# State-space scan over strides of four steps, with its matrices built in the feed-forward parts, in a three-layer model on one core

## What is computed

```python
lam_bar = exp(lam * delta)                    # 64 groups x 64 complex states, diagonal
b_bar   = ((lam_bar - 1) / lam)[..., None] * b   # 64 states from 16 channels
state_t = lam_bar * state_{t-1} + b_bar @ u_t # 272 steps
y_t     = real(c @ state_t) + d * u_t         # 16 channels from 64 states
g       = gelu(y);  out = g * sigmoid(g @ w_glu + b_glu)
```

## Time and profile before

| | us |
|---|---|
| median of 3 runs (lowest, highest) | 3449.91 (3440.37, 3450.88) |
| the profiled execution's own time | 3458.53 |
| its span | 3456.4 |
| PE busy, PEld busy | 3290.6 (95%), 2918.0 (84%) |
| DVE, ACT, POOL busy | 1871.3 (54%), 1418.2 (41%), 732.3 (21%) |

### The profile page before, as it was taken

How to read it: one execution, slowest core, us unless ns; L and a number is a source line. 1 busy time by engine, 2 the same in 40 slices (tenths; PEclk the granted TensorE clock), 3 DMA queues, 4 the chain that set the end, 5 groups by cost and what they waited for, 6 DMA issues and landing times.

```text
span 3456.4 us, 53985 instructions
## 1 busy us (share of the span) xinstructions
PE 3290.6 (95%) x20542; PEld 2918.0 (84%) x20542; DVE 1871.3 (54%) x2405; ACT 1418.2 (41%) x2093; POOL 732.3 (21%) x754
## 2 busy tenths in 40 slices
PE   6989999999999998999999999977778999999999
PEld 6977898989898996799998989865545898989897
DVE  4535544444445544554444445599956545454444
ACT  4334543334345434443333333544335433333343
POOL 2100030303031100012121213257731030303030
PEclk9987999999999998899999999987768999999999
DMA  5541445554554453255555554522102455455544
GB/s 192 181 184 37 180 185 195 189 191 180 194 195 176 178 191 122 93 188 188 184 188 194 189 188 182 210 87 74 49 25 88 181 193 189 180 192 194 192 176 167
DMA packets 41616, 567.02 MB, mean 164 GB/s; under 512 B 4512, under 2 KB 4640, under 8 KB 7168
## 3 DMA queue, kind: packets, MB, share of 16 engines
q1 hardware_dynamic: 39536, 557.49, 44.0%
q0 software_dynamic: 704, 4.68, 0.4%
q10 hardware_dynamic: 1232, 2.88, 0.2%
HBM read 562.93 MB, written 2.10 MB: 163 GB/s over the span
## 4 chain that ended last, share of the span: by engine, by line
PE 83%; DVE 8%; issue 5%; ACT 2%; POOL 1%; DMA 0%; ACTq 0%; DVEq 0%; POOLq 0%; SPq 0%
PE bank L549 82%; DVE mprod L1585 1%; DVE w_lo L1303 1%; DVE mprod L1591 1%; DVE zr L1598 1%; DVE ph L1569 1%; DVE zi L1599 1%; DVE ph L1564 1%; PE bank L596 1%; DMA raw<-stream 0%; PE bank L734 0%; POOL cssb L1833 0%; DVE nsum L1664 0%; ACT prob L1062 0%; PE bank L862 0%
## 5 line engine op out<-in xcount | busy, mean ns | idle before, releaser
L549 PE MATMUL bank<-xg_hi,w_hi 128*128 128x256 f32 (+1 forms) x4352 | 1232.6, 283 | 8.4 <-DVE w_lo L1303 6.3
L549 PE MATMUL bank<-xg_lo,w_hi 128*128 128x256 f32 (+1 forms) x4352 | 1233.1, 283 | 0.0
L549 PE MATMUL bank<-xg_hi,w_lo 128*128 128x256 f32 (+1 forms) x4352 | 1232.1, 283 | 0.0
L927 ACT ACTIVATE w_hi<-raw 128x1024 fp32r<-128x1024 f32 x552 | 554.1, 1051 | 877.3 <-PE bank L549 877.0
L1297 DVE TENSOR_TENSOR w_lo<-raw,w_hi 128x1024 fp32r<-128x1024 f32 x480 | 572.6, 1235 | 557.4 <-ACT w_hi L938 557.1
L549 PEld LDWEIGHTS bank<-xg_hi,w_hi 128*128 128x128 f32 x4352 | 829.4, 191 | 24.4 <-issue 21.2
L549 PEld LDWEIGHTS bank<-xg_hi,w_lo 128*128 128x128 f32 x4352 | 830.8, 191 | 0.0
L549 PEld LDWEIGHTS bank<-xg_lo,w_hi 128*128 128x128 f32 x4352 | 824.4, 189 | 0.7
L938 ACT ACTIVATE w_hi<-raw 128x1024 fp32r<-128x1024 f32 x480 | 482.5, 1053 | 764.7 <-PE bank L549 764.7
L549 PE MATMUL bank<-w_hi,act_hi 128*128 128x512 f32 x1920 | 749.7, 390 | 14.9 <-DVE act_lo L1677 13.1
L549 PE MATMUL bank<-w_lo,act_hi 128*128 128x512 f32 x1920 | 748.0, 390 | 0.0
(11 more groups left out here) (277 smaller groups left out, 2044.2 us busy)
## 6 DMA issues: line engine op xcount, KB each, us to landing
raw<-stream SPq DMA_DIRECT2D x264, 2048.0 KB, 7.7
x<-xrow ACTq DMA_DIRECT2D x4, 512.0 KB, 13.4
gfb<-gfin POOLq DMA_DIRECT2D x2, 1024.0 KB, 5.5
out<-x SPq DMA_DIRECT2D x4, 512.0 KB, 6.5
cbias_sb<-cbias SPq DMA_DIRECT2D x2, 768.0 KB, 9.6
bm<-bmat POOLq DMA_DIRECT2D x1, 1024.0 KB, 6.7
cm<-cmat POOLq DMA_DIRECT2D x1, 1024.0 KB, 13.4
tab<-tables ACTq DMA_DIRECT2D x1, 768.0 KB, 5.0
```

The costliest lines, as they stand in the source:

```text
L549: return pe.matmul(o, a, b, start=start, stop=stop, skip_group_check=True)
L927: act.activation(hi[j][:, 8 * h:8 * h + 8, :], raw[r][:, 8 * h:8 * h + 8, P * j:P * j + P], ACT.Copy)\
```

## The change

1. **A stride of four steps.** The scan runs over 68 strides, not 272 steps. For each group of 4 pairs (one channel tile i) five things are needed: a drive matrix (4 inputs into the state, 2x4x[128,128]), sine, cosine and decay of 68 angles for the 4 pairs, a matrix of the inputs within the stride (`near`, 4x[128,128]) and a read-out of the state before the stride (`far`, 2x4x[128,128]). d*u goes into `near`.
2. **These tables are built in the FFN parts.** In each of the two first layers, after the mixer, POOL computes powers and constants (`ssm_powers`, 69 steps that each wait for the one before; ACT's exponentials, sine and cosine stand in `widened` of the output projection, and DVE has one reciprocal); then in each FFN part POOL builds the tables of one i (`ssm_build`, 22 such steps): the first before the FFN's hidden tiles, the others after those of the part before. ACT makes sine and cosine ahead of `ups`. Behind `ups` PE does 8 transposes and 8 matmuls, DVE adds d, ACT copies the results out; SP stores 3376 floats a partition (1.7 MB) to DRAM and loads 0.66 MB of inputs for the next. The constants at the start are gone.
3. **The loop of the second block** has 20 slots, one whole projection tile each (8 u, 2 k, 2 v, 8 q). Slot s also holds `drive(s-1)`, `read_out(s-3)` and DVE's and POOL's work on group s-1 (the same operations as for one pair before, on 272 elements, without the angles). `u` goes to DRAM and comes back in the layout of the stride (one store and four loads from ACT's queue, with ACT waiting for the store), and so does y. SP loads each group's tables (0.52, 0.42 and 0.79 MB).
4. **GELU** moves to slots 14 to 17, in 8 operations per step over strided views; the squares of the queries and their sums go into the slots, tile by tile.
5. **Attention part:** the gate's half tiles stand in steps -2 to 5. The norm of the SSM half runs in steps 9 to 17, its sums by PE. The sums for the attention half are made by PE per tile; its root, scaling and parts stand ahead of ACT's and DVE's splits of the output projection, which PE begins with the SSM half.

The diff, cut to its core:

```diff
+STRIDE = 4
+NQ = L2 // STRIDE
+PT = 4
+MT = STRIDE * NQ
@@ sync
+                def store_tables(i):
+                    sp.wait_ge(tabs_out, i + 1)
+                    sp.dma_start(stabs[i][:, 0:TAB_F], tabs[:]).then_inc(tabs_stored, 16)
+                    sp.dma_start(stabs[i][:, TAB_F:TAB_ALL]..., fmat[:, :, :, 1:POWERS, :]...).then_inc(tabs_stored, 16)
...
+            for s in range(1, 10):
+                if s + 1 < T2:
+                    sp.wait_ge(bu_done, s)
+                    load_drive(s + 1)
+                if s % 2 == 1:
+                    chunk((s + 1) // 2 + 2)
+                if 0 <= s - 2 and s + 1 < T2:
+                    sp.wait_ge(state_ready, s - 1)
+                    load_trig(s + 1)
+                if 0 <= s - 3 and s - 1 < T2:
+                    sp.wait_ge(y_done, s - 2)
+                    load_readout(s - 1)
@@ tensor
+            def ssm_tables(i):
+                pe.wait_ge(mats_ready, i + 1)
+                for e in range(2):
+                    for j in range(PT):
+                        pe.transpose(bank[4 + e][:, P * j:P * j + P], gmat[:, e, j, :], ident)
+                for j in range(PT):
+                    for e in range(2):
+                        last = mm(bank[6][:, P * j:P * j + P], sb_re_im[:, e, j, :], fmat[:, e, j, 0:STRIDE, :]..., e == 0, e == 1)
+                last.then_inc(mats_built, 1)
...
                 ups(T0, n)
+                if i0 is not None:
+                    ssm_tables(i0)
                 widened(T0 + T_UP, 0, None, hidden_ready(0))
...
+            def drive(i):
+                pe.wait_ge(u_landed[i % 2], 64 * (i // 2) + 64)
+                pe.wait_ge(drv_landed[i % 2], 16 * (i // 2) + 16)
+                if i >= 2:
+                    pe.wait_ge(bu_out, i - 1)
+                for e in range(2):
+                    for j in range(PT):
+                        last = mm(bank[4 + 2 * (i % 2) + e][:, NQ * j:NQ * j + NQ], drv[i % 2][:, e, j, :], u[:, i, NQ * j:NQ * j + NQ], True, True)
+                last.then_inc(bu_done, 1)
...
+            for s in range(SLOTS):
+                tile(T, s % 2, s % 2, ...)
+                if s == 0:
                     spread(4)
+                if 1 <= s < T2 + 1:
+                    drive(s - 1)
+                if 3 <= s < T2 + 3:
+                    read_out(s - 3)
...
             pe.wait_ge(kn_ready, 2)
-            for s in range(H2 + 3):
+            for s in range(GLU0, H2 + 3):
+                if 0 <= s - GLU0 < 8:
+                    gate_half((s - GLU0) // 2, (s - GLU0) % 2)
@@ scalar
-            act.activation(dl[:], par_at("log_step", 0, PAIRS), ACT.Exp).then_inc(ssm_exp, 1)
-            ...
             split(0, 0, 0, 0)
...
+            def feed(i):
+                act.wait_ge(evac_done, evacuated(T_B2 + i))
+                act.dma_start(urow[i], us[i % 2][:]...).then_inc(us_stored, 16)
+            def feed_back(i):
+                act.wait_ge(us_stored, 16 * i + 16)
+                for r in range(STRIDE):
+                    act.dma_start(u[32 * r:32 * r + 32, i, :]..., turned[r]).then_inc(u_landed[i % 2], 16)
...
+            for s in range(SLOTS):
+                split_after(T_B2 + s)
+                if s < T2:
+                    feed(s)
+                if 4 <= s < T2 + 4:
+                    y_out(s - 4)
+                if s < T2:
+                    feed_back(s)
+                if 4 <= s < T2 + 4:
+                    y_back(s - 4)
@@ vector
+            for s in range(SLOTS):
+                if s < K0:
+                    input_tile(s)
...
+                split_after(T_B2 + s)
+                if s < 2 * NC:
+                    final_normed(s)
+                if 1 <= s < T2 + 1:
+                    products(s - 1)
+                    driving(s - 1)
+                    sums(s - 1)
@@ gpsimd
                 pool.wait_ge(olo_ready, OTHERS * l + OTHERS)
                 pool.wait_ge(onlo_ready, HB * l + HB)
-                pool.tensor_tensor(scratch, eps, eps, ALU.add)
+                ssm_powers(l)
+                ssm_build(FCH * l)
+                for f in range(FCH - 1):
+                    hidden(T0 + T_FFN, l * H_LAYER, f)
+                    ssm_build(FCH * l + f + 1)
+                hidden(T0 + T_FFN, l * H_LAYER, FCH - 1)
+                pool.wait_ge(tabs_stored, 32 * FCH * l + 32 * FCH + 1)
                 pool.dma_start(gfb[:], gfin).then_inc(gfb_landed, 16)
-                ffn(T0 + T_FFN, l * H_LAYER)
```

More of the change, by code:

```diff
@@ L92 @@
 _at = 0
[L93 removed]
+for _n, _w in [("ident", P), ("halves", P), ("cos", S), ("sin", S), ("mask", 384), ("dist", 384), ("steps", 68), ("live", 68),
+               ("eye4", 32)]:
     TABLES[_n] = (_at, _w)
@@ L115, in mixed_tile, with build @@
     return g + 8 if g < 8 else g - 8
-def build(nc, stream, params, tables, tables2, cbias, xrow, gfin, metaT, bmat, cmat, out):
+def build(nc, stream, params, tables, tables2, cbias, xrow, gfin, metaT, smat, out, stabs, urow, yrow):
     at = [(nc.sbuf_base + 63) // 64 * 64]
@@ L178, in build @@
     tab2 = tab[:, a2:a2 + NTAB2]
-    dist2, steps = tab2[:, 0:416], tab2[:, 416:NTAB2]
-    region = [free_at, free_at + 30 * 4 * S]
+    dist2 = tab2[:, 0:416]
+    region = [free_at, free_end]
     sqj = [place(f"sqj{i}", [P, W], where=region) for i in range(2)]
-    xgf = [place(f"xgf{i}", [P, W], where=region) for i in range(2)]
     diag = place("diag", [P, 2, P], where=region)
@@ L622, in widened @@
                         if n is not None and c and t == 0:
+                            if c == 1 and tables is not None:
+                                pe.wait_ge(tabs_out, tables)
                             pe.wait_ge(evac_done, evacuated(Tb + 4 * c - 1))
@@ L1824, in _ @@
             pool.wait_ge(tab_landed, 16)
-            with pool.Fori(0, DEPTH) as l:
+            for l in range(DEPTH):
                 T0 = l * TILES_LAYER
@@ L1997, in small_params @@
     put("ssm2_g", columns(a["ssm_out_g_2"][0]))
-    put("ssm_d", columns(a["ssm_d_2"][0]))
+    put("ssm_d4", np.tile(a["ssm_d_2"][0].reshape(PAIRS, 32).T, (STRIDE, 1)))
     put("b_glu", columns(a["b_glu_2"][0]))
```

979 lines of the change are left out of this document (576 added, 403 removed).

## The result

The changed kernel took 3406.3 us (median of 4 runs, 3396.1 to 3410.2) against 3450.4 us (median of 4, 3440.4 to 3455.9): a ratio of 0.9871, 95% interval [0.9851, 0.9892], 1.3% faster. The forecast was 3326 us (3.6% faster) with a range of 3292 to 3378: the sign was right, the gain a third of the forecast, the time 80 us above it and outside the range. The profiled execution after took 3396.1 us (span 3394.3 us) where my sum stood at 3334.6 us; these 61.5 us are what has to be explained.

What follows compares the result with a forecast made beforehand. It took the kernel as PE-bound with one 250 us DVE-bound SSM stretch. 3458.5 - 148 (stage 412 to 264) - 7.5 (start) + 17.6 (PE tables) + 12 (POOL late) + 2 (sine) = 3334.6, times 0.9975: 3326 us, range 3292 to 3378.

Steps and rivals of the forecast that it cites:

- Slots 0 to 8: Second block's new loop: first slot 6 us, seven more at 10.3, and 2 for the lead-in, 80 us.
- slots 9 to 12: Second block's new loop: four slots with read-outs or k's small matmuls at 7.5 us each, 30 us.
- each waits for the others in order; I take 10.3: Slot time in the new loop: PE, DVE, ACT and u's round trip lie between 8.6 and 9.8 us; 10.3 taken.
- (10.4 + 8.6) / 2: New loop: u there 10.4 us after its tile, PE asking one tile (8.6 us) later, so a slot is 9.5 us.
- I take 0.13: Small 68-column matmuls on PE at 0.13 us each: 8 for the drive 1.0 us, 12 for the read-out 1.6.
- Rival (a): Slots bound by u's transfer, 8 us longer, at half clock: 13 to 16 us a slot, 3345 to 3366 us; chance 0.25.
- Slots 13 to 19: Seven slots with a q tile, 5.5 us plus 0.3 of sums each, 41 us, and 6 us of GELU uncovered.
- attention to the output projection: Second block's attention: gate halves, steps with gate 31 us, ten without gate 52 at lost clock, and the tail: 107 us.
- Start: Kernel start without the constants: ACT's first split at 17 us instead of 25.89, -7.5 us.
- Tables on PE: FFN parts: 16 small matmuls or transposes and a wait on PE, 2.2 us eight times, +17.6 us, uncovered.
- GpSimd late: First table build of each layer delays POOL's first hidden tile for DVE: 6 us, twice, +12 us (0 to 70).
- rival (c): POOL late in the first FFN parts and PE's table work dearer, each stop 5 us more: 3400 to 3440 us; chance 0.08.

Runs made afterwards that it cites:

- e10: e4 with u collected a slot later, its dependent work another slot later, weights asked for before tables, GELU one slot later, PE's FFN loop written out: 3352.4 us, ratio 0.9702.
- e4: e3 with the drive, products, read-out and copy of y one slot later, so u has a whole slot for its trip: 3360.3 us.
- e1: Changed kernel with both turns of u and y through DRAM left out, so the output differs: 3389.9 us.
- e3: Changed kernel with ACT copying y of slot s-4 before it splits the next weight tile, arithmetic kept: 3374.6 us.
- e12: e10 with spare matmuls in attention steps 13 to 17, PE's FFN loop kept as a loop and sixteen 16-column matmuls ahead of it: 3365.2 us, ratio 0.9742.
- e6: e4 with ACT waiting for no store of its own slot, and PE's FFN loop over the second and third part written out: 3373.7 us.
- e8: e4 with ACT waiting for no store of its own slot, and one transpose replacing PE's table-building work in the FFNs, output wrong: 3344.7 us.
- e9: e4 with ACT waiting for no store of its own slot, and table loads cut to 16 KB once buffers are filled, output differs: 3355.1 us.

## Why the prediction was wrong

**Slots 0 to 8: 92.8 us, forecast 80; slots 9 to 12: 62 us, forecast 30.** (Slots 0 to 8 end here at the k tile of 2342.5.) This is the step that failed, 45 of the 66 us by which the stage was longer (329.7 us by the forecast's own marks, against 264). What failed was "each waits for the others in order; I take 10.3": I set the sums of four engines beside each other and added a little, without walking through ACT's order. There the read-out's bank hangs on a copy behind a split that waits for PE's tile. And I priced a gap at its own length; it costs its length and then several us at half clock. Nor is "(10.4 + 8.6) / 2" a sum: PE asks for u one tile later in every slot, so a round trip of 10.4 gives 10.4 a slot.

PE's own work was mis-sized too, and that the whole 110 lies near e10's 107.1 without waits is luck. "I take 0.13" for a small float32 matmul: each of them makes two entries of 0.11 us in the trace at full clock, so the twenty cost 4.4 us and not 2.6, and a full slot costs PE 10.5 us and not 8.6 (e4, the row at 2287.60, PE busy 10.50 at clock 1.00). Slots 9 to 12, forecast at 7.5 each, took 10.5, 10.5, 9.2 and 9.0 in e4 at full clock, 39 us and not 30. Against that, the first slots are shorter than 10.3, since their small matmuls are not all there yet.

Rival (a) had the second half (clock 0.78, 13 to 16 us a slot) at 0.25, but for the wrong cause in the main, a round trip 8 us too long. From its tile to its last landing u took 7.2 to 15.5 us, 11.1 in the mean, against the 10.4 I took; the medians of 1.8 and 3.8 us hide last loads of 8.1, 9.2 and 11.4, each beside a load of weights. So the trip was late in some slots (PE waited 10.5 us for it in five), and e1 without any trip gained 15 us where e3's order gained 21. For slots 9 to 12 I had no waits at all. There stood 16 us of them (the key root behind y's stores 6.9, the copy of y 5.0, u 4.2), and three of the four slots ran at clocks of 0.68 to 0.77.

The Trainium skill (TensorE: Matmul & The Clock Gate, "Why this matters for your kernels") had the rule that idle gaps between bursts drop PE to half clock. The runs agree and give it a price here: 2.3 us of gap, 5.5 us longer (e4). The page speaks of longer gaps than these of 2.3 to 2.5 us; here they were enough. Small matmuls without a gap came before a fall too, in two places of three (e12).

**Slots 13 to 19: 54, forecast 47; attention to the output projection: 120.6, forecast 107.** The first six steps took 43.9 us by the intervals of the score maxima (3.9, 11.6, 4.8, 11.8, 6.1, 5.7) where I had 31: PE waited 10.0 us in two places for the low halves of the gate's weights. A different order there was not tried. For slots 13 to 19 the record shows 5.2 us of waits for ACT (copies of v and the key root), and no run tried them. That steps without gate fall to half clock was right; what it costs behind the last score is 9 us (48.3 against 39.6, e10 and e4).

**Start: -10.9, forecast -7.5.** First split at 15.00 where I had 17: ACT waited only for its own first weights, landed at 13.7.

**Tables on PE: +2.65 a part, 21.2, forecast 17.6.** Right mechanism; the rows above have 0.88 us for the transposes and 1.7 for the products (0.11 us per entry of the sixteen, two for each of eight float32 products), so a product costs 0.21 us, not 0.13: the same mistake as in the slots.

**GpSimd late: 0, forecast +12.** Its first build ended 7 us after the first relu (417.6 against 410.7; 8 estimated), and the lateness was as forecast, but PE and DVE never waited. What was mis-sized is the slack: DVE's third relu, which waits for GpSimd's first tile, came 9.7 us after the first (420.44), and GpSimd had that tile done at 420.16. It was met by 0.3 us, in the second layer too (1526.11 for 1526.39): luck, not room.

**Not in the forecast: +12.2** at the jump back of TensorE's loop, three times 4.1 (e6, e8, e12). Nothing in the trace of before shows it: its jump took 71.1. **Also not: -6.0** in the second mixer, which varies by 6 us from kernel to kernel with unchanged code: luck. Between the mixers, the FFNs and the first input tile it was +3.2 in all, where 2 stood for the sine.

Sum of the misses: +66 - 3 + 4 - 12 + 12 - 6 + 1 = 62 us, against the 61.5 to be explained.

The time itself lies in the band of rival (c), 3400 to 3440, at 0.08. Its mechanism did not come: PE never waited for GpSimd, and its table work cost 2.65 us a part and not 5 more.

## What to carry to other kernels

For a loop over several in-order engines, write down for every slot which instruction each engine stands at and what is queued behind it; the sum per engine is only the floor. A copy that frees a bank goes ahead of anything that waits for the bank's user, and an engine that also computes should never wait for a transfer that it has just issued: ask for it one slot, collect it in the next. On TensorE price a gap above its length: in this kernel 2.3 us cost 5.5 in a slot and 2.5 us cost 4.1 at the jump. Look at the late transfers and at what large load stands beside them, not at the median. Spare full-size matmuls are worth a try where TensorE is both the bound and at half clock, with several executions of each kernel, since the clock may stay up without them.

## What the runs showed of the hardware

- A jump back in TensorE's program cost 2.46 us of idle and some 3 us at clock 0.50 in some layouts of the code and nothing in others (71.1 against 73.6 to 76.7 us); shifting the code by sixteen matmuls took it out of one of three places, writing the loop out removed it.
- TensorE's clock fell without a gap, 1 us behind 3.5 us of 16-column float32 matmuls at 100% busy; full-size matmuls then ran at half rate (0.21 us for 0.12) for 3.4 us. In the second of three places with the same padding it stayed at 1.00.
- A 136 KB store that lands in 1.8 us (median) took 8.5 and 11.3 us with the DMA engines 0.8 to 0.9 busy. Loads of 34 KB, and one of 16 KB, that were issued beside a 2 MB load landed with it, after 8 to 9 us (e9), against 2 us otherwise. Four issues on ACT's queue took 1.9 to 2.5 us, 0.5 to 0.6 each, where I had taken 0.73.
- The same attention code takes 134 or 143 us, and a mixer 94 to 100, depending on where the clock falls. Behind the last score it took 48 or 39.6 us with no spare matmuls, and 41 to 42 in the three executions with them.
